# A third set of spare buffers for the expert weights, and a router that runs ahead of the second norm

## What is computed

```
mix = (sigmoid(g_P) * P + sigmoid(g_A) * A) @ W_o
x   = LayerNorm(alpha * x + (1 + gate1) * mix) * ln1_g + ln1_b
u2  = LN(x) * (1 + scale2) + shift2
logits = u2 @ w_router + b_router; top 4 of 32 experts per token, softmax over the 4
expert e: g = min(xb @ wg + bg, 7); up = clip(xb @ wu + bu, -7, 7)
          h = g * sigmoid(1.702 * g) * (up + 1);  y = h @ wd + bd
x   = LayerNorm(alpha * x + (1 + gate2) * sum of weighted y) * ln2_g + ln2_b
```

## Time and profile before

| | |
|---|---|
| median of 3 runs | 1167.73 us |
| profiled execution, its own time | 1166.89 us |
| its span, first to last instruction | 1165.0 us |
| TensorE matmul busy | 1126.5 us, 97% |
| VectorE, ScalarE, GpSimd busy | 345.1, 127.3, 20.1 us |
| mean granted TensorE clock | 0.997 |
| read from HBM | 460.33 MB, mean 396 GB/s over the span |
| DMA share of SP's queue | 94.3% of 16 engines |

### The profile page before, as it was taken

How to read it: one execution, slowest core, us unless ns; L and a number is a source line. 1 busy time by engine, 2 the same in 40 slices (tenths; PEclk the granted TensorE clock), 3 DMA queues, 4 the chain that set the end, 5 groups by cost and what they waited for, 6 DMA issues and landing times.

```text
span 1165.0 us, 13496 instructions
## 1 busy us (share of the span) xinstructions
PE 1126.5 (97%) x5821; PEld 553.7 (48%) x5821; DVE 345.1 (30%) x628; ACT 127.3 (11%) x227; POOL 20.1 (2%) x28
## 2 busy tenths in 40 slices
PE   6999999999999999999999999999999999999996
PEld 4868887454444444444444444444444444444442
DVE  4297963642222211211221112221211121112113
ACT  2113221130001000000000000001000100000001
POOL 0000400000000000000000000000000000000000
PEclk9999999999999999999999999999999999999998
DMA  9999685789999999999999999999999999999994
GB/s 346 387 352 353 242 331 230 283 307 394 426 426 427 425 427 425 429 426 429 434 430 430 431 431 432 432 432 432 432 430 431 432 431 432 432 425 427 426 420 196
DMA packets 53732, 462.01 MB, mean 397 GB/s; under 512 B 5294, under 2 KB 7214, under 8 KB 34746
## 3 DMA queue, kind: packets, MB, share of 16 engines
q1 hardware_dynamic: 50032, 457.19, 94.3%
q10 hardware_dynamic: 3658, 4.20, 1.1%
HBM read 460.33 MB, written 1.05 MB: 396 GB/s over the span
## 4 chain that ended last, share of the span: by engine, by line
PE 75%; DMA 21%; DVE 3%; SPq 1%; issue 0%; ACT 0%; DVEq 0%; ACTq 0%
PE bank L1519 43%; DMA ring<-w_up 19%; PE bank L1502 8%; PE bank L1350 6%; PE bank L1546 4%; PE bank L1287 4%; PE bank L1651 2%; PE bank L1435 2%; PE bank L1344 2%; DMA pool_region<-ln_b 1%; DMA ring<-w_in 1%; PE bank L1540 1%; PE bank L1527 1%; SPq L475 1%; PE bank L1508 1%; PE bank L1375 0%
## 5 line engine op out<-in xcount | busy, mean ns | idle before, releaser
L1519 PE MATMUL bank<-ring,feat_region 128*64 128x512 f32 x2848 | 625.2, 595 | 14.3 <-DMA ring<-w_up 14.3
L1519 PEld LDWEIGHTS bank<-ring,feat_region 128*64 128x64 f32 x2848 | 199.5, 137 | 415.7 <-issue 394.9
L1502 PEld LDWEIGHTS bank<-row_region,ln_tok 128*128 128x128 f32 x1024 | 116.8, 192 | 20.3 <-issue 19.7
L1502 PE MATMUL bank<-row_region,ln_tok 128*128 128x64 f32 x1024 | 121.1, 277 | 0.2 <-DVE row_region L1035 0.2
L1100 DVE TENSOR_TENSOR gate_region<-bank,row_region 128x512 f32<-128x512 f32 x31 | 21.4, 691 | 249.4 <-PE bank L1519 249.4
L1078 DVE TENSOR_SCALAR gate_region<-bank 128x512 f32<-128x512 f32 x31 | 21.4, 691 | 200.9 <-PE bank L1527 200.9
L1090 DVE TENSOR_SCALAR acc_region<-bank 128x512 f32<-128x512 f32 x31 | 21.4, 692 | 170.6 <-PE bank L1527 170.6
L1350 PE MATMUL bank<-feat_region,ring 128*128 128x256 f32 x320 | 70.6, 381 | 0.0
L1546 PE MATMUL bank<-gate_region 64*128 64x512 f32 x264 | 65.9, 616 | 0.8 <-DVE gate_region L1123 0.8
L1350 PEld LDWEIGHTS bank<-feat_region,ring 128*128 128x128 f32 x320 | 60.4, 190 | 10.9 <-issue 3.1
L753 ACT ACTIVATE gate_region<-bank 128x256 f32<-128x256 f32 x31 | 11.9, 383 | 470.1 <-PE bank L1508 470.1
(11 more groups left out here) (240 smaller groups left out, 611.9 us busy)
## 6 DMA issues: line engine op xcount, KB each, us to landing
ring<-w_gate SPq DMA_DIRECT2D x16, 4096.0 KB, 27.6
ring<-w_up SPq DMA_DIRECT2D x16, 4096.0 KB, 30.6
ring<-w_down SPq DMA_DIRECT2D x16, 4096.0 KB, 31.7
ring<-w_gate SPq DMA_DIRECT2D x28, 2048.0 KB, 15.5
ring<-w_up SPq DMA_DIRECT2D x26, 2048.0 KB, 15.2
ring<-w_down SPq DMA_DIRECT2D x26, 2048.0 KB, 17.9
ring<-w_ada SPq DMA_DIRECT2D x8, 2048.0 KB, 15.9
ring<-w_in SPq DMA_DIRECT2D x6, 2048.0 KB, 13.9
```

The source lines that it names most:

```text
L1502: last = nc.tensor.matmul(M_BANK[:, k * CAP:(k + 1) * CAP], u2[:, t, k * P:(k + 1) * P], pick_tok[:, b, t, :], start=t == 0, stop=t == NT - 1)
L1519: last = nc.tensor.matmul(dst[hf * CAP:(hf + 1) * CAP, :], lhs(k0 + k), cols(tiles[k], hf), start=first and k == 0, stop=last_one and k == 3)
```

## The change

- The call that makes the program sets the dynamic DMA scratch to 1024 bytes. A new tensor `ninth` of 16 KB in each partition takes a whole unit.
- There are three extras now, a set of eleven places: `ninth`; `late_rows` with `spare_tile`; `feat_rows` (the region of the normed input's transpose) with `ln_rows`. `x_tok` is an extra no longer. A list gives how many extras are used in each lap over the ring, `EXTRAS = (3, 3, 2, 2, 2, 2, 1, 1)`: eleven places up to u = 21, ten up to u = 61, nine up to u = 79, then eight. `FINE_TURNS` is 4 instead of 3. `x_sel`, `h`, `h_t` and the transposed `u2` move into `gate_region`.
- `ninth` is loaded with unit 8 in the front, right behind ("in", 7). SP's first loads are reordered: units 0 to 3, the first half of `feat_rows`, `late_rows`, unit 4, `ln1_g` and `ln1_b` (moved here from ScalarE's queue), unit 5, `spare_tile`, units 6 and 7 after `mix`, and `ln_rows` when the last statistics of the second norm are there.
- Tile 1 of `mix` has three parts (512, 256 and 256 columns).
- The router works on the first norm's output `z`: TensorE transposes `z` as soon as VectorE has written a half, and the second norm is applied to the logits afterwards (`logits = (raw - mean * scale_row) * rstd + shift_row`, two small VectorE instructions for each tile). The sums over rows come from a matmul behind the first part of `mix`. `u2` itself is made by ScalarE, two 1024-column instructions for each tile, beside the router.
- The 0/1 rows of the four choices are multiplied one by one on TensorE (12 small matmuls in place of 3), so VectorE needn't add them up first.
- The gather of expert 0 is cut in two: its first half ahead of the first gate unit, the second half inside that unit. The transposes of the weights and the seed of tile 1 move into the second gate unit. The filler shrinks from 4 to 3 matmuls, and one of 256 columns is added.
- The loads of `ln2_g` and `ln2_b` wait for 96 used units instead of 48.

```diff
-EXTRA = 2
-WIDE_TURNS = 2
-FINE_TURNS = 3
+FINE_TURNS = 4
+EXTRAS = (3, 3, 2, 2, 2, 2, 1, 1)
...
+def fine_places():
+    place, extra, before = {}, {}, {}
+    holders = {}
+    for lap, count in enumerate(EXTRAS):
+        for n in range(SLOTS + count):
+            u = len(place) + len(extra)
+            if n < SLOTS:
+                holder = place[u] = SLOTS * lap + n
+                holder %= SLOTS
+            else:
+                extra[u] = (n - SLOTS, lap)
+                holder = n
+            before[u] = holders.get(holder)
+            holders[holder] = u
...
+        ninth = sb("ninth", [P, SLOT])
...
+                if u == ("in", 7):
+                    load_extra(SLOTS)
...
-            for m in range(SLOTS - 2):
+            for m in range(4):
                 fill_slot(m)
+            sp.wait_ge(job_done, JOB_POOL)
+            sp.dma_start(feat_rows, source(SLOTS + 2)[:, 0:2, :]).then_inc(extra_landed[2], 16)
             sp.wait_ge(job_done, JOB_POOL + 2)
             sp.wait_ge(router_scaled, 1)
             sp.dma_start(late_rows, source(SLOTS + 1)[:, 0:3, :]).then_inc(extra_landed[1], 16)
+            fill_slot(4)
             sp.wait_ge(merged, KT // 2)
+            for r, w in enumerate((ln1_g, ln1_b)):
+                sp.dma_start(ln_rows[:, r, :], w.to_broadcast([P, D])).then_inc(ld_ln1, 16)
+            fill_slot(5)
             sp.dma_start(spare_tile, source(SLOTS + 1)[:, 3, :]).then_inc(extra_landed[1], 16)
             for m in range(SLOTS - 2, SLOTS):
                 fill_slot(m)
-            sp.wait_ge(u2_ready, 2 * NT)
-            sp.dma_start(ln_rows, source(SLOTS)[:, 0:2, :]).then_inc(extra_landed[0], 16)
-            sp.wait_ge(seeded, 2 * NT)
-            sp.dma_start(x_tok[:, :, :], source(SLOTS)[:, 2:4, :]).then_inc(extra_landed[0], 16)
+            sp.wait_ge(moments_ready, 2 + 2 * NT)
+            sp.dma_start(ln_rows, source(SLOTS + 2)[:, 2:4, :]).then_inc(extra_landed[2], 16)
...
             for b in range(2):
                 u2_t_half(1, b)
+            norm_std(1, 1)
+            u2_tile(1)
+            nc.scalar.activation(small[:, 102:103], eps, ACT.Exp)
...
             for t in range(NT):
                 for k in range(KT):
                     if k % 4 == 0:
-                        pe.wait_ge(u2_ready, 2 * t + k // 4 + 1)
+                        pe.wait_ge(z_ready, 2 * t + k // 4 + 1)
...
+                last.then_inc(logits_done, 1)
                 if t == 0:
-                    keep_busy(4)
+                    pe.wait_ge(scaled_ready, 1)
+                    pe.wait_ge(mix_read, MIX_PARTS)
+                    seed(0)
+                    keep_busy(3)
...
             pe.wait_ge(picked, 1)
-            gather(0).then_inc(gather_done, 1)
-            pe.wait_ge(weight_ready, 1)
...
+            pe.wait_ge(u2_ready, NT)
+            first_gather(0)
+
+            def weights_and_seed():
+                pe.wait_ge(weight_ready, 1)
...
+                pe.wait_ge(gate2_ready, 1)
+                seed(1)
...
+                               between=(lambda: first_gather(1), weights_and_seed)[k] if first and j == 0
+                               else None) \
...
-    nc = bacc.Bacc("TRN2", target_bir_lowering=False, num_devices=1)
+    nc = bacc.Bacc("TRN2", target_bir_lowering=False, num_devices=1, dynamic_dma_scratch_size=1024)
```

More of the change, by code:

```diff
@@ L52 @@
 MATRICES = UNITS // 2
+FINE_TURNS = 4
+EXTRAS = (3, 3, 2, 2, 2, 2, 1, 1)
+EARLY_TILES = 2
 TURN_UNITS = BODY * UNITS
-WIDE_TURNS = 2
-FINE_TURNS = 3
[L56 to L66, removed]
+def fine_places():
[12 more added lines that the diff above has]
+            holders[holder] = u
+    for u in range(len(before), FINE_TURNS * TURN_UNITS):
+        place[u] = u - sum(EXTRAS)
+        before[u] = holders[place[u] % SLOTS]
+        holders[place[u] % SLOTS] = u
+    return place, extra, before
+PLACE, EXTRA_OF, BEFORE = fine_places()
 PIECES = (2, 2, 2, 4, 2, 4)
@@ L90, in fine_fills @@
 def fine_fills():
[L91 to L102, removed]
+    count, landed = list(FILLS), {}
+    for u, place in PLACE.items():
+        if not SLOTS <= place < SLOTS + EARLY_TILES:
+            count[RING[place % SLOTS]] += 1
+            landed[u] = count[RING[place % SLOTS]]
+    return count, landed
+FINE_FILLS, LANDED = fine_fills()
 C_IDENT, C_TRI = 0, 128
@@ L695, in _ @@
                 job(JOB_POOL + n)
[L696 to L699, removed]
             act.wait_ge(y_cleared, 1)
@@ L1456, in keep_busy, with seed @@
                     nc.tensor.matmul(bank[b][:, 0:columns], ident, const[:, 0:columns], start=True, stop=True)
+            pe.wait_ge(row_sums_ready, 2)
+            def seed(t):
+                for n in (2 * t, 2 * t + 1):
+                    nc.tensor.matmul(bank[n][:, :], scaled_ident, x_tok[:, n // 2, (n % 2) * HALF:(n % 2 + 1) * HALF],
+                                     start=True, stop=False)
             for t in range(NT):
@@ new lines, in _ @@
+            keep_busy(1, 3, S)
+            for t in range(NT):
+                pe.wait_ge(picks_ready, t + 1)
+                if t == 0:
+                    for k in range(TOP_K):
+                        nc.tensor.matmul(Y_BANK[:, 0:NE], tri_bf, picks[:, 0, k, :],
+                                         start=k == 0, stop=k == TOP_K - 1)
+                for k in range(TOP_K):
+                    last = nc.tensor.matmul(Y_BANK[:, NE:2 * NE], tri_bf if t else one_bf[:, 0:1].to_broadcast([P, P]),
+                                            picks[:, t, k, :], start=(t, k) == (0, 0), stop=(t, k) == (1, TOP_K - 1))
@@ L1499, in gather, with gather_tile @@
+            last.then_inc(rank_done, 1)
+            def gather_tile(dst, b, k):
+                for t in range(NT):
+                    last = nc.tensor.matmul(dst, u2[:, t, k * P:(k + 1) * P], pick_tok[:, b, t, :],
+                                            start=t == 0, stop=t == NT - 1)
+                return last
             def gather(b):
                 for k in range(KT):
[L1501 to L1503 removed]
@@ L1513, in out_cols, with stream @@
                 return tile[:, hf * HALF:(hf + 1) * HALF]
-            def stream(dst, lhs, tiles, k0, first, last_one, cols=half_cols, tile_done=None):
+            def stream(dst, lhs, tiles, k0, first, last_one, cols=half_cols, tile_done=None, between=None):
                 for k in range(4):
+                    if k == 2 and between is not None:
+                        between()
                     for hf in range(2):
```

291 lines of the change are left out of this document (154 added, 137 removed).

## The result

The changed kernel takes **1170.48 us** (median of 8 runs, 1169.65 to 1175.25) against 1167.79 us for the kernel before (8 runs, 1166.23 to 1168.25). The medians differ by 2.7 us, 0.23%. The ratio over all runs is 1.0039, 95% interval 1.0028 to 1.0050; it is higher than that of the medians since three of the eight runs lie near 1175 us. So the kernel is slower, at or just beyond the 0.2% bound, where 1165.2 us and a range of 1161.0 to 1168.6 were forecast: a small gain came out as a small loss. The profiled execution took 1170.52 us, its span is 1168.6 us, and the mean granted clock is 0.993 (0.997 before).

A forecast was written before the change was run, and what follows sets the result against it. The weights stream was taken to bind in the end, set by when TensorE has used unit 4. Terms -4.9 + 1.4 + 1.0 = -2.5 us on the profiled 1166.89 gave 1164.4, as median 1165.2 us; range 1161.0 to 1168.6.

The forecast's parts named there:

- the moment of unit 4: Expert 0's first down unit: when TensorE has used it sets the weights stream; +1.4 us, bounds -1.8 to +3.
- The extra unit: Weights ring: with eleven places, unit 15 instead of 14 waits for unit 4, so the stream is one unit further; -4.9 us.
- the filler did hold the transposes: Router: tile 1's transposes wait for TensorE's own filler until 235.1 us, 3.3 us after their data.
- the gather came at: End of the router: TensorE starts the gather at 241.75 instead of 242.72 us, -1.0 us.
- the half gather and the seed did cost in expert 0: Expert 0's gate units: half gather 1.9, weights' transposes 0.6 and seed of tile 1 1.8 move in, +4.3 us.
- Rival C: Router's stretch: TensorE's clock falls to 1.2 GHz; first gate matrix up to +7.1 us, at 1170 us; chance 0.08.
- Rival A: Router: filler doesn't bind, tile 1's transposes start with their data, all behind 3.2 us earlier; 1162.0 us; chance 0.20.
- Rival B: Weights stream: extra unit doesn't reach the end, a late piece or hole eats it; -0.5 to +1, 1168.0 us; chance 0.17.
- The narrow place at unit 32: Shrinking ring: first unit whose place was used ten units before; makes it by 1.3 us, so counted at nothing.
- The total of the waits: TensorE's own waits for loads over the kernel: should fall from 14.3 to about 10.4 us.
- The fourth turn: Fourth written-out turn: 24 units as 2 MB loads in place of twelve of 4 MB; +1.0 us, bounds 0 to 1.5.

The follow-up runs named there:

- warm: Changed kernel with more filler: two matmuls of 454 columns for one of 256 behind tile 1's logits, one of 454 more ahead of the gather; 1165.90 us.
- filler_logits_only: Changed kernel with only the first filler of warm: two matmuls of 454 columns behind tile 1's logits instead of one of 256; 1165.84 us.
- warm_two_extras: As warm, but two extras in all eight laps, so ten places instead of eleven, without the loads into feat_rows and ln_rows; 1170.65 us.
- no_gap_filler: As seed_back, without the three filler matmuls between the seed of tile 0 and the transposes of tile 1; 1162.50 us.
- filler_gather_only: Changed kernel with only the second filler of warm: one matmul of 454 columns more ahead of the gather; 1167.13 us.
- before_no_filler: Kernel before the change without its filler, four matmuls of 454 columns and one of 256; 1175.50 us.
- warm_three_turns: As warm, but three turns written out instead of four, with ring laps (3, 3, 3, 3, 2, 2); 1165.29 us.
- seed_back: As warm, but the seed of tile 1 replaces the filler behind tile 1's logits and leaves the second gate unit; 1164.77 us.

## Why the prediction was wrong

**The mechanism was right: the moment of unit 4 sets the stream, and the stream the end.** The table above is that sentence measured.

**The extra unit.** -4.9 was forecast, -4.75 measured. `ninth` cost nothing in the front: DMA's hole at 116 us took it up, and TensorE's block of 64 matmuls at 141 us starts 119.2 us behind the one at 22 us in both kernels.

**The moment of unit 4: the step that failed.** +1.4 us was the term, with -1.8 to +3 as its bounds; it measured +6.2 (274.35 for 268.16 us). Of this, 0.55 is the later start of the whole profiled execution (22.60 for 22.05 us), 4.0 are the clock, as warm shows, and 1.6 are the work, which answer to the forecast of 1.4. The steps between were right: the filler did hold the transposes (235.34, forecast 235.1), the gather came at 241.96 (241.75), the half gather and the seed did cost in expert 0. What failed is that a smaller filler was priced only as work, and the clock was taken over from the rows of before as 1.00, so that its fall stood in the sum at nothing. There four fillers stood in front of the transposes, and the second seed behind the logits, at 239.69, with 0.1 us between its end and the small matmuls:

```profile
241.77 0.17 PE L1494 MATMUL bank<-attn_region 128*128 128x32 bf16 x1
```

The change took away just that seed and left 1.0 us of idle time in its place. It moved 1.8 us of work out of VectorE's shade and thereby took away what kept the clock up.

**Rival C** was the mechanism: clock 0.50, gather and gate matrix at half speed, 1170 us. I gave it a chance of 0.08, since no row of before showed a fall in that stretch; but the rows showed what stood in the idle places, and that the change emptied one of them. The Trainium skill ("TensorE: Matmul & The Clock Gate", Part 1) lets the clock follow how busy the array was just before; the fall from 1.00 to 0.50 behind the idle time, and none with filler in it in any trace, agree. What I took from that page was a rival, and what I should have taken is a check on every removed matmul.

**The sum without it.** Warm, with the changed kernel's work and the clock up, takes 1165.90 us, filler_logits_only 1165.84; 1165.2 was forecast. With the clock's 4.0 us and the 1.6 for 1.4 put in, the sum gives 1169.4 us against 1170.48 measured. The 1.1 us left are not assigned to anything; a profiled execution and the median of its kernel differ by up to 0.9 us here.

**Rival A** (the filler doesn't bind) is refuted: the transposes stand right behind the filler, 2.9 us after their data, and taking it out brings 2.0 to 2.3 us. **Rival B** (the unit doesn't reach the end) is refuted by warm_two_extras. The narrow place at unit 32 cost at most a few tenths: the DMA share from 300 to 400 us stayed at 1.01, with 425 GB/s (426 before). The total of the waits was forecast at 10.4 us; it is 11.9 in the changed kernel and 10.9 in warm.

**The fourth turn.** +1.0 forecast, 0.6 and 2.1 measured in the medians, 1.2 and 0.9 in the chains at 930 us. The Trainium skill ("DMA: Bandwidth & Descriptors", Anatomy of one DMA) gives about 2 us and then 436 GB/s for one DMA, and it gives this for loads issued from GpSimd, while those here are issued from SyncE. That both sizes would stream alike when loads are queued was my own conclusion from it. The stream speaks against it: from 560 to 680 us it runs at 429 GB/s in warm and no_gap_filler, whose loads there are nearly all of 2 MB, and at 432 GB/s in the two kernels with three turns, whose loads there are of 4 MB. By these rates 24 units would differ by some 0.8 us, an estimate.

## What to carry to other kernels

Where a stream of loads binds in the end, find the moment from which it never pauses again, and count every microsecond of work in front of that moment, even on an engine that later waits. Look at what fills the idle places of TensorE ahead of its next dense stretch: a matmul that is moved out of the shade costs its own time where it goes and may cost the clock where it was. Of filler and useful work that can stand in the same place, put the useful work there, and let filler stand only where no data are waiting behind it.

## What the runs showed of the hardware

TensorE's clock fell in a few short matmuls behind 1.04 us of idle time, and stayed low for 10.2 us of mostly dense float32 work in the changed kernel and 3.4 us in filler_gather_only. In before_no_filler 3.2 us were idle, and it stayed low for 20.5 us. With filler in the same place it stayed at 1.00 in the profiled execution, although the engine was idle for 0.62 and 0.59 us around the gather (filler_logits_only).

Four kernels have times in two groups. Two of them have a fall in their trace: the changed one has five runs at 1169.7 to 1170.5 us and three at 1174.9 to 1175.3, before_no_filler one at 1170.66 and three near 1175.5. In the changed one the mean granted clock of the runs is 0.993 in the lower and 0.990 in the upper group, so the upper one spent more time at the lower level. That it is a second such stretch of 10 us in the same place, as in before_no_filler, is likely by the size of the step and wasn't seen in a trace of that kernel. The other two have the idle time filled: filler_logits_only with two of ten runs at 1167.4 and 1167.7, and warm_three_turns, whose router is that of warm, with three of twelve at 1167.9 to 1168.2. These five have a mean clock of 0.996 where the rest of their kernels has 0.997 to 0.998, the value of the profiled execution of filler_gather_only with its fall of 3.4 us. So the filler seems not to hold the clock up in every execution; where it fell in these five wasn't seen in a trace. All 22 runs of warm and seed_back stayed in one group.

With the dynamic DMA scratch at 1024 bytes and a further weight buffer of 16 KB in each partition, the loads streamed at 431 GB/s, as before (432).
